# A decoder layer with expert retrieval: the token in PSUM for 104 dots, block 1's query first in each quarter, rows between the parts of a retrieval, and block 0's V rows ahead of block 1's pairs

## The reference

```python
q = (xt @ w_query).reshape(T, 8, 2, 128)
s = einsum('thcd,hckd->thck', q, sub_keys)          # 8 heads, 2 halves, 128 keys
top_s, top_i = top_k(s, 16)
cand_s = top_s[:, :, 0, :, None] + top_s[:, :, 1, None, :]
best_s, pos = top_k(cand_s, 16)                     # 16 experts per head, 128 per token
gate = softmax(best_s)
u = take(expert_u, ic);  h = gelu(einsum('cd,ced->ce', xc, u))
vv = take(expert_v, ic); out = einsum('ce,ced->cd', gate * h, vv)
x = layer_norm(ALPHA * x + out)
```

## Time and profile before

| | |
|---|---|
| median of 3 runs | 1624.45 us (1623.74 to 1626.84) |
| the profiled execution | 1616.41 us, span 1614.6 us |
| PE busy | 1300.6 us, 81% of the span |
| DVE busy | 1140.6 us, 71% |
| POOL busy | 735.1 us, 46% |
| ACT busy | 270.3 us, 17% |
| moved by DMA | 603.45 MB, mean 374 GB/s |
| of it by POOL's indirect DMAs | 536.91 MB |

### The profile page before, as it was taken

How to read it: one execution, slowest core, us unless ns; L and a number is a source line. 1 busy time by engine, 2 the same in 40 slices (tenths; PEclk the granted TensorE clock), 3 DMA queues, 4 the chain that set the end, 5 groups by cost and what they waited for, 6 DMA issues and landing times.

```text
span 1614.6 us, 11652 instructions
## 1 busy us (share of the span) xinstructions
PE 1300.6 (81%) x3512; PEld 625.1 (39%) x3512; DVE 1140.6 (71%) x2715; ACT 270.3 (17%) x766; POOL 735.1 (46%) x645
## 2 busy tenths in 40 slices
PE   8979979986879896787878787777777879787886
PEld 5466436533334554333333332333333323333332
DVE  1349999877888869977676768676767686764544
ACT  0100000122222111121212121212121212121111
POOL 0005456677656455553544343544444445343430
PEclk9989999998989998897989888999998898898899
DMA  9948789899889978999999999999999999999992
GB/s 340 390 149 319 306 287 357 349 407 354 283 286 342 353 279 336 421 422 422 422 421 422 421 421 422 421 422 421 422 421 421 421 422 422 422 422 422 421 422 118
DMA packets 125710, 603.45 MB, mean 374 GB/s; under 512 B 12624, under 2 KB 14928, under 8 KB 76368
## 3 DMA queue, kind: packets, MB, share of 16 engines
q0 software_dynamic: 92160, 536.91, 82.4%
q1 hardware_dynamic: 33488, 65.80, 11.1%
HBM read 600.57 MB, written 2.10 MB: 373 GB/s over the span
## 4 chain that ended last, share of the span: by engine, by line
DMA 40%; DVE 24%; PE 22%; POOL 7%; issue 4%; SPq 1%; ACT 1%; DVEq 0%; POOLq 0%
DMA arena<-uv,idx 38%; PE W L512 7%; POOL arena L475 5%; DVE arena L1095 5%; PE ACC L512 4%; PE W L547 2%; PE W L553 2%; PE W L791 2%; DVE xs L1087 2%; DVE arena L1073 2%; DVE cand L1341 1%; DVE cand L1343 1%; DVE sel L1345 1%; PE ACC L499 1%; DMA arena<-peer_w_query 1%
## 5 line engine op out<-in xcount | busy, mean ns | idle before, releaser
L1095 DVE SCALAR_TENSOR_TENSOR arena<-arena,xs 128x1024 f32<-128x1024 f32 x384 | 466.6, 1226 | 294.2 <-DMA arena<-uv,idx 292.4
L461 POOL DMA_INDIRECT arena<-uv,idx x384 | 432.7, 1127 | 527.4 <-PE W L512 305.9
L512 PE MATMUL W<-arena,fdiag 128*128 128x512 f32 x1024 | 504.2, 653 | 143.8 <-ACT fdiag L1025 143.7
L475 POOL DMA_INDIRECT arena<-uv,idx x232 | 272.9, 1176 | 287.6 <-DVE idx L1351 125.8
L512 PEld LDWEIGHTS W<-arena,fdiag 128*128 128x128 f32 x1024 | 210.3, 209 | 437.0 <-issue 256.1
L512 PE MATMUL ACC<-arena,fdiag 128*128 128x512 f32 x512 | 250.5, 651 | 73.6 <-ACT fdiag L1025 73.6
L512 PEld LDWEIGHTS ACC<-arena,fdiag 128*128 128x128 f32 x512 | 105.3, 209 | 218.9 <-issue 129.0
L1025 ACT ACTIVATE fdiag<-ident,gate 128x128 f32<-128x128 f32 x384 | 123.2, 390 | 356.8 <-DVE gate L1102 356.0
L1073 DVE SCALAR_TENSOR_TENSOR arena<-arena,xs 128x1024 f32<-128x1024 f32 x128 | 151.6, 1225 | 22.9 <-DMA arena<-uv,idx 22.2
L547 PE MATMUL W<-arena 128*128 128x512 f32 x320 | 142.5, 601 | 8.5 <-DMA arena<-w_in 7.8
L1087 DVE SCALAR_TENSOR_TENSOR xs<-arena,gate,xs 128x1024 f32<-128x1024 f32 x80 | 102.7, 1284 | 29.6 <-DMA arena<-uv,idx 23.3
(11 more groups left out here) (184 smaller groups left out, 884.1 us busy)
## 6 DMA issues: line engine op xcount, KB each, us to landing
arena<-w_in SPq DMA_DIRECT2D x13, 2048.0 KB, 12.9
arena<-peer_w_query SPq DMA_DIRECT2D x8, 2048.0 KB, 17.0
arena<-uv,idx POOLq DMA_INDIRECT x616, 25.7
arena<-w_out SPq DMA_DIRECT2D x4, 2048.0 KB, 15.8
arena<-w_in SPq DMA_DIRECT2D x4, 512.0 KB, 6.6
out<-xs SPq DMA_DIRECT2D x4, 512.0 KB, 7.9
arena<-xT SPq DMA_DIRECT2D x1, 1536.0 KB, 19.9
xs<-x SPq DMA_DIRECT2D x1, 1536.0 KB, 17.1
```

Of the source, the lines that this page charges most:

```text
L461: pool.indirect_dma_start(out=fused[slot], out_offset=None, in_=uv, in_offset=bass.IndirectOffsetOnAxis(ap=idx[:, E + n:E + n + 1], axis=0 ...
L475: pool.indirect_dma_start(out=ring[r], out_offset=None, in_=rows, in_offset=bass.IndirectOffsetOnAxis(ap=idx[:, e:e + 1], axis=0), element ...
L512: last = nc.tensor.matmul(sum_of(b)[:, half * HW:(half + 1) * HW], fdiag[:, n % ND, :], fused[n % NS][:, D + half * HW:D + (half + 1) * HW ...
L1095: STT(out=fused[slot][:, 0:D], in0=fused[slot][:, 0:D], scalar=1.0, in1=xs[:, b, :], op0=ALU.mult, op1=ALU.mult, accum_out=hid[:, E + n:E ...
```

## The change

1. **Token in PSUM.** ACT copies block 0's token (two 128x512 activations, `token_to_psum`) into the PSUM tensor X. The first 104 dots take it from there, the other 24 from SBUF as before. X is next written by the out projection of block 1, which now also waits until dot 103 is done.
2. **Block 1's query first.** In each quarter of wave 1's query, PE does the four pieces for block 1 alone (128 tokens, `query_one`), then pieces for blocks 2 and 3 together (256 tokens, `query_two`); block 1's keys are scored after the first of these. The scores of blocks 2 and 3 of a quarter come after the next quarter's block 1 query.
3. **Rows within retrievals.** DVE does 10 rows instead of 18 ahead of `retrieve(1, 0)`, three rows between each two of the three parts of both retrievals, and 8 rows between the retrievals; 18 are left behind them.
4. **V rows ahead of pairs.** All rows through V31 are issued before pair 0. The groups V22 to V31 take quads A, D, B in turn (`LAST_QUADS`), where they took A and B. The first six pairs take slots 1, 3, 4, 0, 2, 5, so that only the fourth waits for quad D.

```diff
+LAST_QUADS = [A_QUAD, D_QUAD, B_QUAD, A_QUAD, D_QUAD, B_QUAD, A_QUAD, B_QUAD, A_QUAD, B_QUAD]
 for j in DVE_GROUPS:
-    WHERE["V", j] = (D_QUAD, B_QUAD)[j % 2] if j < 22 else (A_QUAD, B_QUAD)[j % 2]
+    WHERE["V", j] = (D_QUAD, B_QUAD)[j % 2] if j < 22 else LAST_QUADS[j - 22]
+TOKEN_IN_X = 104
+PAIR_SLOTS = [1, 3, 4, 0, 2, 5] + list(range(6, NS))
...
-            early = {("V", 25): (0, 3), ("V", 28): (3, EARLY)}
+            early = {("V", 31): (0, EARLY)}
...
-                slot = n % NS
+                slot = PAIR_SLOTS[n % NS]
                 if n == 0:
                     pool.wait_ge(mixer_ready, 2 * NB)
+                elif n == 3:
                     for r in range(12, RING):
                         pool.wait_ge(slot_used[r], uses_of(3))
...
                     if b > 1:
                         pe.wait_ge(x1_taken, 2 * b)
+                    else:
+                        r, used_by = slot_of("U", TOKEN_IN_X - 1)
+                        pe.wait_ge(slot_used[r], used_by)
...
+            def query_1():
+                pe.wait_ge(x1_taken, 2 * NB)
+                for s in range(WQ):
+                    n = 4 + 5 * s
+                    query_one(1, s, n, 1)
+                    if s:
+                        score_two(s - 1)
+                    query_two(s, 0, n + 1)
+                    pe.wait_ge(query_taken, n + 1)
+                    score_keys(s, 4 + 3 * s, q_one)
+                    for i in range(1, 4):
+                        query_two(s, i, n + 1 + i)
+                score_two(WQ - 1)
...
+            def token_to_psum():
+                act.wait_ge(x1_ready, 1)
+                for half in range(2):
+                    last = nc.scalar.activation(X_BANKS[half], xs[:, 0, half * HW:(half + 1) * HW], ACT.Copy)
+                last.then_inc(token_in_psum, 1)
...
             def dot(e):
                 if e == 0:
-                    dve.wait_ge(x1_ready, 1)
+                    dve.wait_ge(token_in_psum, 1)
+                token = X[:] if e < TOKEN_IN_X else xs[:, 0, :]
...
-                STT(out=ring[r], in0=ring[r], scalar=1.0, in1=xs[:, 0, :], op0=ALU.mult, op1=ALU.mult,
+                STT(out=ring[r], in0=ring[r], scalar=1.0, in1=token, op0=ALU.mult, op1=ALU.mult,
...
-            rows(18)
-            retrieve(1, 0)
-            rows(14)
-            retrieve(1, 1)
-            rows(E + len(DVE_GROUPS) * HALF - taken[0])
+            rows(10)
+            for q, n in ((0, 8), (1, E + len(DVE_GROUPS) * HALF)):
+                best_keys(1, q)
+                rows(3)
+                best_pairs()
+                rows(3)
+                best_experts(1, q)
+                rows(min(n, E + len(DVE_GROUPS) * HALF - taken[0]))
```

More of the change, by code:

```diff
@@ new lines, in query_0, with query_one @@
+                    query_one(0, s, s, 0)
+                    pe.wait_ge(query_taken, s + 1)
+                    score_keys(s, s, q_one)
+            def query_one(w, s, n, b):
+                slot, count = wslot(w, WIN + WOUT + s)
+                pe.wait_ge(w_landed[slot], count)
+                wait_query_bank(n)
+                for i in range(4):
+                    for k in range(KD):
+                        last = nc.tensor.matmul(W[:, 2 + n % 2, i * P:(i + 1) * P], wts[slot][:, k, i * P:(i + 1) * P],
+                                                actT[:, k, b * P:(b + 1) * P], start=(k == 0), stop=(k == KD - 1))
+                last.then_inc(query_ready, 1)
@@ new lines, in query_two, with wait_query_bank @@
+            def query_two(s, i, n):
+                slot, count = wslot(1, WIN + WOUT + s)
+                wait_query_bank(n)
+                for k in range(KD):
+                    last = nc.tensor.matmul(W[:, 2 + n % 2, 0:2 * P], wts[slot][:, k, i * P:(i + 1) * P],
+                                            actT[:, k, 2 * P:4 * P], start=(k == 0), stop=(k == KD - 1))
+                last.then_inc(query_ready, 1)
+            def wait_query_bank(n):
+                if n in (1, 2, 3) or n > 5:
+                    pe.wait_ge(query_taken, n - 1)
```

110 lines of the change are left out of this document (52 added, 58 removed).

## The result

The changed kernel took 1638.23 us (median of 7 runs, 1632.90 to 1640.58) against 1626.37 us for the kernel before on the same chip (7 runs, 1623.74 to 1628.71): ratio 1.0062, 95% interval 1.0039 to 1.0086. I had forecast 1620.3 us, faster. The experiments show that this is half of the story: on another chip of the same type the same change makes the kernel 0.55% faster. Two executions of later experiments, both of part 1 with one memset, ran at a lower granted clock (0.735 and 0.81, where all others have 0.90 or more) and took 1722.9 and 1652.38 us; they are left out of the medians.

The account below looks back on a forecast made before the run. The prediction took the start of the DMA-bound pair stream to set the end. Faster row issues (-6.5 us) and a later pair 0 (+2.3) gave -4.2 us, so the median 1624.45 becomes 1620.3 us, range 1612 to 1628.

Parts of the forecast that it names:

- What bounds the kernel: From about 646 us DMA moves 421 to 422 GB/s; the end follows the start of the unbroken pair stream.
- Part 1, the mechanism: Beside the first 104 dots a row issue takes 0.94 us instead of 1.99; the dots get no dearer.
- Part 1, the places: Two stretches before 400 us pass the faster row issues on: 6.5 us earlier in sum, bounds 0 and 11.7.
- the first place: At 240 to 245 us DVE's waits for rows vanish: 2.2 us earlier, bounds 0 and 3.5.
- the second place: From 320.22 to 389.94 us POOL's 49 row issues come faster: 4.3 us gained, bounds 0 and 8.2.
- Parts 2 to 4: From 528.87 us: scores and retrievals come earlier, yet pair 0 goes out 2.3 us late, bounds -1 and +6.
- the number to beat: Pair 0 at 620.8 us, the start that would equal the pair stream of the kernel before.
- The sum: -6.5 + 2.3 = -4.2 us on the profiled execution, carried to the median: 1624.45 becomes 1620.3 us, 0.26% faster.
- Pairs too late: Pair 0, now behind every V row, starts too late at the end of the chain: 1628.3 us; chance 0.15.
- No arrival: Upstream DMA is already full, so faster issues give 2.2 us at most, cancelled by +2.3: 1624.5 us; chance 0.25.
- More than I count: Both upstream gains reach their upper bounds, 11.7 us, and the stretch from 528.87 us comes out even: 1612.8 us; chance 0.14.
- A dearer dot: The dot from PSUM costs 1284 ns, not 1225, so 104 cost DVE 6.1 us: 1626.4 us; chance 0.03.

Follow-up runs that it names:

- part 1 with one memset: Kernel before with block 0's token in PSUM for 104 dots, plus one small POOL memset behind each U row issue: 1607.64 and 1607.28 us.
- part 1 alone: Kernel before with only block 0's token in PSUM for 104 dots: ratios 1.0073 and 1.0033 on chips with late signals, 0.9934 on one without.
- the runs meant to take the load away: Changed kernel with row DMAs that fetch only half of each row: 1597.73, 1600.29 and 1596.18 us.
- parts 1 and 2: Kernel before with block 0's token in PSUM and block 1's query first, rows and pairs in the old order: 1633.21 us, ratio 1.0025.

## Why the prediction was wrong, by its own steps

- **What bounds the kernel.** Right on both kinds of chip: 421 to 422 GB/s from the 17th slice on, and the end follows the start of the pair stream.
- **Part 1, the mechanism.** Right: issues at 0.94 us beside the dots (the group of 232 row issues falls from a mean of 1176 ns to 1044), dots at 1217 ns. The Trainium skill (SBUF — State Buffer, "Who interferes with whom") says that a DVE instruction with one SBUF input does not contend with GpSimd. Both traces agree: the issue takes 0.94 us beside such an instruction. By the same section's inference that descriptor generation needs the write interface, part 1 would give 0; the 1.99 us beside the dots with two SBUF inputs, and the fall of the mean, speak against it.
- **Part 1, the places.** On chip 5, counted from the first indices (125.62 us before, 121.60 after; this first difference lies ahead of any row, in the 20 profiles the place varies from 121.6 to 126.1 us with no order by kernel, and I don't count it): PE's first scores of block 1 (308.79 us, before 316.63) come 3.8 us earlier (I had 2.2 at the first place, 3.5 as the bound), block 1's sum at 392.81 us, against 406.30, comes 9.5 us earlier. So the second place gave 5.7 (I had 4.3). The first is more than DVE's waits since PE's wait of 3.54 us went with it: the 3.8 lie above my bound of 3.5, so the size of this term was too small. ln1 of block 3 is 8.5 us earlier with the whole change, and 10.6 with part 1 alone (I had 6.5).
- **Parts 2 to 4.** Right in every step. Behind the end of ln1, in us, predicted and then measured on chip 5: block 1's scores 18.7 and 18.6; first indices 42.8 and 42.3; second indices 78.0 and 77.1; pair 0 94.2 and 93.5. Against the number to beat (620.8 - 528.87 = 91.9) that is 1.5 us late; I had 2.3. The medians of chip 5 say 2.0 (1607.79 - 1605.77), chip 2 says 4.8 and chip 4 2.2 between the same two kernels, differences that the intervals of the ratios, 3 us and more to either side, do not tell from 0.
- **The sum, the step that failed.** I had -4.2 us on the profiled execution, and this kind of chip gives -8.9 (0.9945). Part 1's term was too small, as above. The failure on the chip of the comparison is the next sentence, "That execution ran 8.0 us under the median, so on the median 1624.45 - 4.2": it takes the 8 us for a constant that the change leaves alone, and with it "I let the whole stretch move by that amount". The profile of before fits the chips without late signals, and the forecast was measured on one with them. There part 1 is not -6.5 but +11.9 and +5.4 us (chips 2 and 4), and its profiles hold more late signals than those without it. That the 8 us themselves are late signals in the kernel before is likely but not shown, since it was not profiled on such a chip.
- **How much of it the late signals are.** Between the two profiles of the changed kernel (chips 1 and 5), the stretch from the first indices to the end of ln1 of block 3 is 423.2 us (547.14 - 123.97) and 394.7 us (516.32 - 121.60). The four late signals of the chain are 21.7 of these 28.5 us. The rest I have not assigned; part of it is PE at a granted clock of 0.50, the lower of its two levels, behind such a wait, as in the window below, just after the one at 260.7 us.

```profile
263.00:264.00 1.00, 1.00 (x7) 1.00 (x6) 1.00 (x3) 0.00 (x0) 0.60 (x1) 0.50 0.05 20
```

- **What stays open.** Why signals come late on some chips, and what a full DMA has to do with it. That a full DMA goes with the late signal at 260 us is shown (6 of 6 against 0 of 3), but so does part 1; that it is the cause is not shown, since the runs meant to take the load away met only chips without late signals, and the full DMA of the pair stream brings none. Late signals at 137 us are in kernels with and without part 1 alike. That the engines waited for their instructions is not borne out by the trace: it has one packet of an instruction queue between 244 and 246 us, and none between 250 and 262 us.
- **A rival that no run tests: the recording.** In the nine profiles with late signals the trace itself has gaps. Of the 1118 to 1163 semaphore updates that PE, ACT, DVE and POOL make between 130 and 700 us, 149 to 239 are not in it; between 700 and 1590 us, where no signal is late, at most 6 are missing. (These counts are from the kept traces, updates recorded against instructions that make one.) In the eleven profiles without late signals none is missing in either stretch. So late signals and lost records go together in chip and in time. Whether one thing holds up both, or the recording itself delays the signals, is open.
- **The rivals.** None of mine had this. "Pairs too late" had the right sign on the chips with late signals, but for another reason: pair 0 goes out 91.1 us behind the end of ln1 on chip 1 and 93.5 on chip 5, and I had 94.2. "No arrival" is refuted by the 8.5 us of chip 5. "More than I count" comes nearest on chip 5 (-11.7, measured -8.9), and says nothing of the other kind. "A dearer dot" is refuted by 1217 ns.

## What to carry to other kernels

Before a difference is carried from one profile to a median, ask whether the profile belongs to the same population: one that is faster than every timed run does not, and what the runs have more may react to the change. A difference under 1% should be measured on several chips, against the kernel before on each, since here the same edit is worth -0.66% on one and +0.73% on another. And a wait whose releaser the profile does not know is worth a look at what it waits for: in the changed kernel's profile all the long ones wait for one engine. Count the records too: where some are missing, the trace says less about who released whom.

## What the runs showed of the hardware that I had not expected

- Chips of one type differ: the unchanged kernel has medians of 1615.20, 1616.67 and 1615.84 us on three of them, and 1627.31 and 1628.18 us on two others (1626.37 on chip 1).
- On the latter, instructions that wait for PE start up to 17 us after PE's record has ended (17.1 us at 401.3 us, parts 1 and 2 on chip 4). ACT, DVE and POOL see it. DVE's signals come late too, more seldom (four, by 1.2 to 5.1 us, between 385 and 394 us in the profile of the changed kernel on chip 2). All lie between 130 and 682 us.
- A memset of 128x128 on POOL takes 0.22 us and shortens the gap to the next issue from 0.30 to 0.16 us, so that one memset per issue lengthens the pitch only from 1.24 to 1.33 us (I had expected 1.45).
